# FFN 2's gate and up projections by blocks: seven products for eight, with two of the weight sums made by accumulating transfers

## The reference

```python
def swiglu(h, w_gate, w_up, w_down):
    return (jax.nn.silu(h @ w_gate) * (h @ w_up)) @ w_down
...
x = x + 0.5 * g1 * swiglu(modulate(rms_norm(x, norm_ffn1), sh1, sc1), ffn1_w_gate, ffn1_w_up, ffn1_w_down)
x = x + g2 * token_mixing(modulate(rms_norm(x, norm_mix), sh2, sc2), ...)
h = modulate(rms_norm(x, norm_ffn2), sh3, sc3)
x = x + 0.5 * g3 * swiglu(h, ffn2_w_gate, ffn2_w_up, ffn2_w_down)
return rms_norm(x, final_norm)
```

## Time and profile before

| | us |
|---|---|
| median of 3 runs (1163.82 to 1164.69) | 1164.69 |
| the profiled execution | 1163.01 |
| its span | 1161.2 |
| PE busy in the span | 1145.9 (99%) |
| VectorE busy | 625.5 (54%) |
| ScalarE busy | 451.7 (39%) |
| POOL busy | 58.9 (5%) |
| TensorE's granted clock | 0.997 of full |

### The profile page before, as it was taken

How to read it: one execution, slowest core, us unless ns; L and a number is a source line. 1 busy time by engine, 2 the same in 40 slices (tenths; PEclk the granted TensorE clock), 3 DMA queues, 4 the chain that set the end, 5 groups by cost and what they waited for, 6 DMA issues and landing times.

```text
span 1161.2 us, 16214 instructions
## 1 busy us (share of the span) xinstructions
PE 1145.9 (99%) x5730; PEld 969.9 (84%) x5730; DVE 625.5 (54%) x1051; ACT 451.7 (39%) x709; POOL 58.9 (5%) x86
## 2 busy tenths in 40 slices
PE   8899999999999999999999999999999999999997
PEld 7788888888888998888888888899888888888887
DVE  5766666666555666776565566756433333333332
ACT  5233332332222357665555566434322222222232
POOL 3301000000000000010001010000000000000000
PEclk9999999999999999999999999999999999999999
DMA  9567566556555423343343442341333333333332
GB/s 312 162 219 243 181 218 204 174 184 211 172 172 167 110 63 102 91 125 86 90 120 96 111 117 72 91 139 37 97 98 101 90 98 101 90 93 94 99 113 74
DMA packets 221149, 151.45 MB, mean 130 GB/s; under 512 B 5078, under 2 KB 202916, under 8 KB 221108
## 3 DMA queue, kind: packets, MB, share of 16 engines
q1 hardware_dynamic: 217108, 138.76, 39.8%
q0 software_dynamic: 3280, 9.79, 3.2%
q10 hardware_dynamic: 720, 2.36, 0.6%
HBM read 148.73 MB, written 4.52 MB: 132 GB/s over the span
## 4 chain that ended last, share of the span: by engine, by line
PE 91%; DVE 2%; SPq 2%; issue 1%; DMA 1%; ACT 1%; POOL 0%; DVEq 0%; POOLq 0%; ACTq 0%
PE bank L1492 28%; PE bank L1494 28%; PE bank L1493 28%; PE bank L1827 2%; PE bank L1820 1%; SPq L446 1%; PE bank L1843 1%; PE bank L1815 1%; PE bank L1842 1%; DMA raw<-in_ffn_w_gate_dram 1%; SPq L465 1%; DMA adas<-in_ada_w_dram 1%; SPq L459 0%; DVE hL L1010 0%; DVE tmp L1005 0%
## 5 line engine op out<-in xcount | busy, mean ns | idle before, releaser
L1492 PE MATMUL bank<-hH,wH 128*128 128x512 f32 (+1 forms) x1072 | 413.2, 385 | 3.6 <-DVE hL L1010 3.1
L1494 PE MATMUL bank<-hH,wL 128*128 128x512 f32 (+1 forms) x1072 | 409.0, 382 | 0.0
L1493 PE MATMUL bank<-hL,wH 128*128 128x512 f32 (+1 forms) x1072 | 408.8, 381 | 0.0
L617 ACT ACTIVATE wH<-raw 128x1024 fp32r<-128x1024 f32 (+1 forms) x169 | 176.2, 1042 | 500.2 <-PE bank L1494 500.2
L944 DVE TENSOR_TENSOR wL<-raw,wH 128x1024 fp32r<-128x1024 f32 (+1 forms) x169 | 203.4, 1204 | 280.3 <-ACT wH L617 279.7
L1492 PEld LDWEIGHTS bank<-hH,wH 128*128 128x128 f32 x1072 | 201.6, 188 | 44.4 <-issue 5.1
L1494 PEld LDWEIGHTS bank<-hH,wL 128*128 128x128 f32 x1072 | 201.5, 188 | 39.1
L1493 PEld LDWEIGHTS bank<-hL,wH 128*128 128x128 f32 x1072 | 201.8, 188 | 37.7
L1492 PE MATMUL bank<-actH,wH 128*128 128x512 f32 (+1 forms) x332 | 126.9, 382 | 0.0
L1494 PE MATMUL bank<-actH,wL 128*128 128x512 f32 (+1 forms) x332 | 126.6, 381 | 0.0
L1493 PE MATMUL bank<-actL,wH 128*128 128x512 f32 (+1 forms) x332 | 126.6, 381 | 0.0
(11 more groups left out here) (204 smaller groups left out, 1188.6 us busy)
## 6 DMA issues: line engine op xcount, KB each, us to landing
adaw<-in_ada_w_dram SPq DMA_DIRECT2D x28, 1024.0 KB, 6.0
raw<-in_ffn_w_gate_dram SPq DMA_DIRECT2D x43, 512.0 KB, 3.8
raw<-in_ffn_w_up_dram SPq DMA_DIRECT2D x43, 512.0 KB, 3.8
raw<-in_mix_w_in_dram SPq DMA_DIRECT2D x41, 512.0 KB, 3.8
raw<-in_ffn_w_down_dram SPq DMA_DIRECT2D x32, 512.0 KB, 3.7
adas<-in_ada_w_dram SPq DMA_DIRECT2D x16, 512.0 KB, 8.2
raw<-in_ffn_w_down_dram SPq DMA_DIRECT2D x16, 384.0 KB, 3.4
raw<-in_mix_w_out_dram SPq DMA_DIRECT2D x8, 512.0 KB, 3.7
```

The source lines that it names most:

```text
L617: nc.scalar.activation(wH[s][:, :n * P], raw[s][:, :n * P], ACT.Copy).then_inc(hi_done, 1)
L1492: T.matmul(o, a[0], b[0], start=start, stop=False)
L1493: T.matmul(o, a[0], b[1], start=False, stop=False)
L1494: return T.matmul(o, a[1], b[0], start=False, stop=stop)
```

## The change

The units `U_GU2` to `U_GU2 + 7` stay as they are (`DIRECT` = 2 pairs of hidden tiles: tiles 0, 1, and in their second place 11, 12: the pair of tile i is now i and i + 11). The other 18 tiles are computed in `N_TWOS` = 9 rounds. A round t takes the tiles i = 2 + t and i + 11, gate and up, and multiplies by blocks: the contraction is cut in halves of 512 features, the tokens in halves of 256, the columns in tile i and tile i + 11. The 2 x 2 by 2 x 2 block product is made of seven products and sums instead of eight products. A product is, for gate and for up, four tiles deep: 2 x 4 x 3 = 24 matmuls of 128x256, and gate and up lie in the two halves of one bank. `ORDER_P` = 1, 2, 5, 6, 7, 3, 4 is their order, `B_P` their banks.

What each product needs:

- **Input blocks.** Products 1 and 2 (and 3) read blocks of `hH` and `hL` as they are. Products 6, 7, 4 and 5 read sums of blocks. POOL adds high and low part of each of the four blocks (`whole`, into `hB`), DVE makes four sums (`token_sums`), ACT and DVE split them again (`t_high`, `t_low`), into `tH` and `tL`, and product 5's in the place of block 12 of `hH` and `hL`. This is done once, beside the direct units.
- **Weight blocks.** Products 1, 2 and 4 use a block of the weights as loaded. Products 5 and 7 need the sum of two: SP loads one block, and POOL then issues two transfers that add the other to it in the slot (`weight_sums`, `accum_op=ALU.add`). Products 6 and 3 need the sum of product 5 with block 1 and then with block 2: DVE adds them in place (`next_r`). So a round has five loads (`LOADS`), each of two transfers of 256 KB, into four raw slots, two sums by transfers and two by DVE. Slots 2 and 3 lie in the part of `actH` and `actL` that is written last.
- **Outputs.** ACT copies products 1 and 5 out of PSUM (`kept`), DVE adds the others in seven steps (`block`), ACT takes the silu (`gates`), DVE multiplies (`multiply`), and high and low part follow (`act_high`, `act_low`).

The code is written out in full, with no loop in the program. Three pairs of `wH` and `wL` take the products' weights in turn. Down's first turn is taken out of its loop, since two of its units have a home in `tH` and `tL`, and it waits for the hidden tiles in their new order. Four semaphores of the relative table on POOL become one, `table_moved`.

The core of the diff:

```diff
+    ORDER_P = (1, 2, 5, 6, 7, 3, 4)
+    B_P = {1: 4, 2: 7, 5: 5, 6: 6, 7: 0, 3: 1, 4: 2}
+    N_BL, N_TWOS = len(ORDER_P), HF - DIRECT
+    LOADS = (1, 2, 5, 7, 4)
+    N_LOAD, W_SLOTS, RAW_SLOTS = len(LOADS), 3, 4
...
+        def sp_ffn_by_blocks(sp):
...
+            for l in range(N_LOAD * N_TWOS):
+                t, p = l // N_LOAD, LOADS[l % N_LOAD]
+                i = DIRECT + t
+                if l < 2:
+                    sp.wait_ge(lo_done, U_DN2 - 1 + l + FREE)
+                elif l == 2:
+                    sp.wait_ge(t_lo, 3)
+                elif l >= RAW_SLOTS:
+                    t0, p0 = (l - RAW_SLOTS) // N_LOAD, LOADS[(l - RAW_SLOTS) % N_LOAD]
+                    if p0 in (1, 2):
+                        sp.wait_ge(r_made, 2 * t0 + p0)
+                    else:
+                        sp.wait_ge(w_lo, N_BL * t0 + ORDER_P.index(3 if p0 == 5 else p0) + 1)
+                for m in range(2):
+                    k0, tile = {1: (0, i), 2: (DT // 2, i), 4: (DT // 2, i + HF), 5: (0, i + HF), 7: (0, i)}[p]
+                    src = tiles_of(ws[m], slice(tile * P, (tile + 1) * P), DT // 2, k0)
+                    sp.dma_start(raw_slot(l)[:, m, :].rearrange("p (k n) -> p k n", k=DT // 2), src
+                                 ).then_inc(w_in[l % RAW_SLOTS], 16)
...
+            def weight_sums(t, p):
+                l = N_LOAD * t + LOADS.index(p)
+                pool.wait_ge(w_in[l % RAW_SLOTS], 32 * (l // RAW_SLOTS + 1))
...
+                for m, w in enumerate((ffn2_w_gate, ffn2_w_up)):
+                    pool.dma_start(raw_slot(l)[:, m, :].rearrange("p (k n) -> p k n", k=DT // 2),
+                                   tiles_of(w, slice(at, at + P), DT // 2, k0), accum_op=ALU.add).then_inc(w_summed[p], 16)
...
+            def w_high(n):
+                l, p = load_of(n), ORDER_P[n % N_BL]
+                if p in (6, 3):
+                    act.wait_ge(r_made, 2 * (n // N_BL) + 1 + (p == 3))
+                elif p in (5, 7):
+                    act.wait_ge(w_summed[p], 32 * (n // N_BL + 1))
+                else:
+                    act.wait_ge(w_in[l % RAW_SLOTS], 32 * (l // RAW_SLOTS + 1))
...
+                elif n >= W_SLOTS:
+                    act.wait_ge(p_done, n - W_SLOTS + 1)
+                nc.scalar.activation(by_two(w_slot(n)[0]), raw_slot(l), ACT.Copy).then_inc(w_hi, 1)
...
+            def next_r(t, q):
+                n, r = N_BL * t + 2 + q, raw_slot(N_LOAD * t + 2)
+                dve.wait_ge(w_lo, n + 1)
+                V.tensor_tensor(r, r, raw_slot(N_LOAD * t + q), ALU.add).then_inc(r_made, 1)
...
+            def two_by_blocks(t):
+                for at in range(N_BL):
+                    n = N_BL * t + at
+                    if n + 2 < N_PROD:
+                        w_low(n + 2)
+                    else:
+                        prep_home(U_DN2 + n + 2 - N_PROD)
+                    if at < 2:
+                        next_r(t, at)
+                    if t and at == 0:
+                        block(t - 1, 6)
+                        multiply(t - 1, 0)
+                    if t and at == 2:
+                        multiply(t - 1, 1)
+                        act_low(t - 1, 0)
+                    if t and at == 3:
+                        act_low(t - 1, 1)
+                    for step in {4: (0, 1), 5: (2, 3), 6: (4, 5)}[at] if at >= 4 else ():
+                        block(t, step)
...
+                for n in range(N_PROD):
...
+                    pe.wait_ge(w_lo, n + 1)
+                    wh, wl = w_slot(n)
+                    h, l = moving(p)
+                    for m in range(2):
+                        for k in range(DT // 2):
+                            cols = slice((m * DT // 2 + k) * P, (m * DT // 2 + k + 1) * P)
+                            ins = three(bank[:, B_P[p], HALF[m]], (wh[:, cols], wl[:, cols]), (h[:, k, :], l[:, k, :]),
+                                        k == 0, k == DT // 2 - 1)
+                    ins.then_inc(p_done, 1)
```

More of the change, by code:

```diff
@@ L63, in hybrid_block @@
     U_GU2 = U_OUT + DT
-    U_DN2 = U_GU2 + 2 * FT
+    HF, DIRECT = FT // 2, 2
+    U_DN2 = U_GU2 + 4 * DIRECT
     U_END = U_DN2 + 3 * DT
@@ L348, in hybrid_block @@
         out_sent = sem("out_sent")
+        w_summed = {p: sem(f"w_summed{p}") for p in (5, 7)}
+        w_in = [sem(f"w_in{q}") for q in range(RAW_SLOTS)]
+        r_made = sem("r_made")
+        w_hi = sem("w_hi")
+        w_lo = sem("w_lo")
+        p_done = sem("p_done")
+        h_whole = sem("h_whole")
+        t_sum = sem("t_sum")
+        t_hi = sem("t_hi")
+        t_lo = sem("t_lo")
+        kept = sem("kept")
+        c_made = sem("c_made")
+        gated = sem("gated")
+        multiplied = sem("multiplied")
         def head_rows(h):
@@ L599, in _ @@
                         biases_a(i)
+                if n == 4:
+                    pool.wait_ge(hL_done, 5 * DT)
+                    for q in range(4):
+                        whole(q)
+                    for t in range(N_TWOS):
+                        weight_sums(t, 5)
+                        weight_sums(t, 7)
         @block.scalar
@@ new lines, in gate_up_by_blocks, with silu, hi @@
+            def gate_up_by_blocks():
+                u0 = U_GU2
+                def silu(i, k):
+                    act.wait_ge(prod_done[1][k // 2], i + START)
+                    act.wait_ge(unit_done, i * 4 + u0 + k + 1)
+                    nc.scalar.activation(sg[:, k // 2, :], bank[:, k, :], ACT.Silu).then_inc(silu_done[1][k // 2], 1)
+                def hi(i, j):
+                    act.wait_ge(prod_done[1][j], i + 1 + START)
+                    nc.scalar.activation(actH[:, i + HF * j, :], pr[:, j, :], ACT.Copy).then_inc(actH_done[1], 1)
+                for j in range(2):
+                    prep_home(u0 + N_FIRST + j, u0 + (1, N_FIRST)[j])
+                    silu(0, 2 * j)
+                for j in range(2):
+                    hi(0, j)
+                prep(u0, 4, 1, 2)
+                silu(1, 0)
+                prep(u0, 4, 1, 3)
+                hi(1, 0)
+                t_high(6, 3)
+                t_high(7, 2)
+                t_high(4, 4)
+                w_high(0)
+                silu(1, 2)
+                w_high(1)
+                t_high(5, 1)
+                hi(1, 1)
+                for t in range(N_TWOS):
+                    two_by_blocks(t)
+                gates(N_TWOS - 1, 1)
+                for j in range(2):
+                    act_high(N_TWOS - 1, j)
@@ L1654, in body @@
                             f = k0 + q
-                            ins = three(bank[:, 5 + j, :], tile((u0 + k) % 2, q), (actH[:, f, :], actL[:, f, :]),
+                            cols = slice(q * P, (q + 1) * P)
+                            w = [part[:, cols] for part in home(u)] if isinstance(i, int) else tile((u0 + k) % 2, q)
+                            ins = three(bank[:, 5 + j, :], w, (actH[:, f, :], actL[:, f, :]),
                                         f == 0, f == FT - 1)
@@ L1663, in body @@
                             T.transpose(bank[:, B_ADA, :rows], modrows, ident[:rows, :rows]).then_inc(ada_sum, 1)
-                if ada:
-                    body(0)
-                with pe.Fori(int(ada), DT // 2 - 1) as i:
+                body(0)
+                with pe.Fori(1, DT // 2 - 1) as i:
                     body(i)
```

238 lines of the change are left out of this document (222 added, 16 removed).

## The result

The changed kernel takes **1190.58 us** (median of 4 runs, 1190.47 to 1192.33) against 1164.69 us before (1163.82 to 1165.23): ratio 1.0228, 95% interval 1.0214 to 1.0242, 25.9 us slower. The forecast was +12.4 us and 1177. The direction and the range held; the size was less than half of what came.

What follows compares the result with a forecast made beforehand. TensorE's streaming bounds the kernel; the products alone save 14.4 us, but a 4.9 us start stall, turns of 22.8 and a 2.0 stall before down make +12.4, 1177 us on the median's level; 8-in-10 range 1154 to 1204.

Steps and rivals of the forecast that it cites:

- The ring: Wait cycle through SP, POOL, ACT and DVE before each round's product 5: 16.6 us + A a turn, against TensorE's 20.16.
- transfers of 512 KB, two in a row take 3.8 + 2.0 = 5.8 us: SP's loads for products 2 and 5 after X: 3.8 us to land one, 2.0 more movement for the second.
- X: End of product 3's low part on DVE, which frees a slot; each turn is counted from it to the next.
- A: Time from POOL's issue of two accumulating transfers to their landing: 4.2 + 2.0 = 6.2 us; free up to about 3.5.
- DVE's chain 8.4: DVE's nine instructions from product 5's low part to the next X: 8.9 us less 6 overlaps of 0.09, so 8.4.
- high and low 2.29: ACT's high part, 1.06 us, then DVE's low part, 1.23, before product 5 may start.
- Start and tail: First product 5 at 844.3 us, stall 4.9; from the last one to down's first matmul 16.3 to 16.5, stall 2.0.
- The last activations (about 3.5 us ...) are hidden by down's first unit of 5.44 us: At the start of down: the final silu, multiplication, high and low part were to cost TensorE nothing.
- POOL's four additions: Additions of 128x1024 beside the four direct units, 2 x 1277 ns each, from 805.3 to 815.5 us, costing nothing.
- The rivals: Hidden sum, chance 0.09; ring binding a little, 0.16; even, 0.10; slow sums, 0.15; DVE as the bound, 0.04; slow products, 0.02.
- DVE as the bound: Rival: DVE's instructions take 20% longer beside POOL's transfers, a round is 20.5 us, about 1158 us; chance 0.04.
- slow products: Rival: 256-column matmuls don't hold 120 ns; at 188 ns the products would take 284 us, far slower; chance 0.02.

Runs made afterwards that it cites:

- no_sums: Changed kernel without POOL's accumulating transfers, so products 5 and 7 use plain weight blocks without the sum: 1154.19 us, ratio 0.9903 to the kernel before.
- warm: Changed kernel with sixteen dummy matmuls into an idle bank before PE's wait for product 5: 1190.24 us, ratio 1.0231 to the kernel before.
- five_own: Changed kernel with raw slots dealt anew, product 5's load taking the slot of product 2 of the round before: 1168.99 us, ratio 1.0037.
- own_late: five_own's slots, product 7's sum made by VectorE, and product 7's load held until product 5's sums have landed: 1163.32 us, ratio 0.9990.
- seven_waits: Changed kernel with SP issuing product 7's load only when product 5's has landed: 1196.31 us, ratio 1.0279 to the kernel before.
- plain_copy: Changed kernel with POOL's transfers overwriting the slot instead of adding to it: 1173.40 us, ratio 1.0071 to the kernel before.
- Five_first: Changed kernel with SP issuing product 5's load ahead of product 2's from the second round on: 1167.41 us, ratio 1.0024 to the kernel before.
- the last two variants: own_late, 1163.32 us, and own_late with product 5's high and low part made in halves, each behind its own transfer, 1159.52 us.

## Why the forecast was right in kind and short in size

- **The ring.** Right. Idle once a round, before a product 5 (0.7 to 3.0 us from the second round on, and twice 0.5 before a product 6), put down to DVE's low part; ACT waiting for the slot's landing; the matmuls at 120 ns; PE busy 89% (forecast 87%). No_sums shows that nothing else holds the stage, and warm that PE is outside.
- **The term "transfers of 512 KB, two in a row take 3.8 + 2.0 = 5.8 us".** This step failed. It measured 6.92 from X, 1.1 more, eight times over: 9 us of the 11.6 that are missing at down's first matmul (measured +24.0, forecast +12.4). The sum took the 3.8 of the earlier trace rows for a load that runs alone, and the 2.0 for pure movement. Here three loads of 512 KB are issued within 3.2 us, and product 1's, issued 3.4 us before X, is under way until 0.3 to 1.4 us behind it. Product 5's pair goes 1.1 us behind X and takes 5.5 to land, where it takes 3.9 to 4.0 in five_own and own_late. Of the 1.1 us, 0.3 are the time from that landing to POOL's issue, for which the forecast had 0.1 in the whole turn; product 7's load accounts for 0.4 (seven_waits); product 2's, issued as two transfers just ahead, is taken for the last 0.4, as the difference that remains.
- **The term A = 6.2.** 6.54, 0.34 short, eight times: 2.7 us (hand-offs, 0.1 a turn in the forecast, are inside the measured steps). Its parts held: 4.5 measured for the plain pair against 4.2, and 2.0 for the addition. The forecast's sentence that the load for product 7 shares the engines had no number; it needed one.
- **DVE's chain 8.4, high and low 2.29.** 8.34 and 2.32. The order of nine instructions, read with their overlaps, was worth the work.
- **Start and tail.** First product 5 at 33.1 us behind the stage's first unit at 814.84 (forecast 32.5). The last one to down's first matmul 16.6 (16.4). Together 0.8 us. The eight turns took 191.96 us where 181.2 was forecast, so 10.8 of the 11.6 lie in them.
- **"The last activations (about 3.5 us ...) are hidden by down's first unit of 5.44 us".** This step failed too. DVE ends them 7.1 us behind down's first matmul, since five combinations of the last round, two multiplications and a low part of down's weights stand ahead of them in its queue, and PE waits for them before down's second unit, 1.77 us from start to start:

```profile
1063.68 0.50 PE L1869 MATMUL bank<-actH,tH 128*128 128x512 f32 x1 [1.37 <-DVE actL L1441]
```

All variants have it, no_sums with 1.74 too, and before has not. With the 24.0 of the stage that is 25.8, against the 25.9 of the medians.
- **POOL's four additions.** Forecast 2 x 1277 ns each, measured 2894 ns, done 11.5 us after they start; still hidden, so the price of this error was nothing.
- **The rivals.** A stood at 6.5, between the 5.1 and 8 of the forecast; DVE as the bound and slow products are excluded by no_sums. The Trainium skill's fit, "DMA: Bandwidth & Descriptors", section "Anatomy of one DMA — SWDGE (gpsimd) path", gives an estimate of 2.6 us for 256 KB; plain_copy's transfers landed in 3.8 at the median, so the measurement decides for the rows.

The choice that cost most was one that the prediction named and didn't price: product 5's load stands behind product 2's on SP, "though its own slot was free one step earlier". Five_first shows that this place in the queue is worth 23 of the change's 26 us.

## What to carry to other kernels

When a change puts a round trip between engines and DMA queues, write the ring down step by step and compare its turn with the bound engine's; then look on each queue for a transfer that is ready but stands behind a wait. Price a transfer of the ring by rows in which as many bytes are under way as will be beside it, and if there are none, bound it by adding the movement of each neighbour; three 512 KB loads around an accumulating pair stretched it here from 6.5 to 9.8 us. Freeing the ring's transfer earlier helps only if its neighbours don't move with it: hold back those that have time. After each step look again at what ends the wait: in the last two variants it was a plain load, no longer the sums.
